# Router logits from unnormalised rows, their products moved into the memory attention, and result rows added by GpSimd

## What is computed

```python
x = layer_norm(DEEPNORM_ALPHA * x + memory_cross_attention(x, mem, w_q, w_kv, w_o), ln_g[l, 1], ln_b[l, 1])
# o = softmax(q k^T / 16) v for 4 heads of 256; returns o @ w_o
s = jax.nn.sigmoid((xf @ w_router).astype(jnp.float32))        # (512, 32)
sel = s + b_router
# best of 8 groups by its two largest sel; the two best experts in that group; gates = s normalised
x = layer_norm(DEEPNORM_ALPHA * x + y, ln_g[l, 2], ln_b[l, 2])  # y: gated sum of two SwiGLU experts
```

## Time and profile before

| | us |
|---|---|
| median of 3 runs (1113.65 to 1114.56) | 1114.0 |
| the profiled execution, whole | 1116.74 |
| its span, first to last instruction | 1115.0 |
| TensorE busy | 1041.0 (93%) |
| VectorE, ScalarE, GpSimd busy | 343.8, 251.8, 95.8 |
| mean granted clock of TensorE | 0.984 |

### The profile page before, as it was taken

One profiled execution on the slowest core, in us unless ns is written; L12 is line 12 of the kernel. 1 busy time (PEld: TensorE's weight loads), 2 busy tenths in 40 slices (PEclk: granted clock), 3 DMA queues, 4 the chain that ended last, 5 costly groups with the idle time before them and its releaser, 6 DMA issues.

```text
span 1115.0 us, 15720 instructions
## 1 busy us (share of the span) xinstructions
PE 1041.0 (93%) x6594; PEld 521.4 (47%) x6594; DVE 343.8 (31%) x730; ACT 251.8 (23%) x510; POOL 95.8 (9%) x137
## 2 busy tenths in 40 slices
PE   9999999999998999999999899999999999788896
PEld 4444455567655554566544743333333333233332
DVE  0179622334555645203216511111111111011105
ACT  2431122234445520013402111111111111011123
POOL 2000100000000000100000211111111111111111
PEclk9999999999999999999999899999999999999999
DMA  8012320221122150543833899999999999999994
GB/s 279 26 54 76 114 77 2 77 71 42 43 77 97 58 189 1 214 203 129 301 133 125 309 393 419 423 419 421 419 418 422 414 416 416 414 417 416 420 416 175
DMA packets 57462, 265.73 MB, mean 238 GB/s; under 512 B 7122, under 2 KB 8274, under 8 KB 32560
## 3 DMA queue, kind: packets, MB, share of 16 engines
q1 hardware_dynamic: 51200, 255.49, 57.8%
q0 software_dynamic: 4960, 8.15, 2.0%
q10 hardware_dynamic: 1232, 1.08, 0.3%
HBM read 256.56 MB, written 16.25 MB: 245 GB/s over the span
## 4 chain that ended last, share of the span: by engine, by line
PE 42%; DMA 9%; DVE 5%; ACT 2%; issue 1%; DVEq 0%; SPq 0%; ACTq 0%
PE cpair L2042 10%; PE bank L2052 8%; PE tpair L2042 6%; PE bank L1882 2%; PE bank L1862 2%; DMA keys<-in_w_exp_up 2%; DMA ring<-in_w_exp_down 2%; DMA ar<-in_w_exp_down 2%; DMA xT<-in_w_exp_up 2%; DMA ring<-in_w_exp_up 2%; PE bank L2024 2%; DVE hs L2471 2%; PE tpair L1882 1%; ACT hs L2268 1%; PE bank L1855 1%; PE cpair L1882 1%
## 5 line engine op out<-in xcount | busy, mean ns | idle before, releaser
L2042 PE MATMUL cpair<-ring,xgT 128*64 128x512 f32 x344 | 113.5, 593 | 5.0 <-DMA avq<-in_w_exp_up 2.6
L2471 DVE TENSOR_TENSOR hs<-cpair,hs 64x512 f32<-64x512 f32 x21 | 14.6, 693 | 247.8 <-ACT hs L2268 247.8
L2268 ACT ACTIVATE hs<-cpair 64x512 f32<-64x512 f32 x21 | 12.4, 589 | 230.9 <-PE cpair L2042 230.9
L2042 PEld LDWEIGHTS cpair<-ring,xgT 128*64 128x64 f32 x344 | 35.4, 137 | 55.8 <-issue 55.8
L922 PE MATMUL bank<-xT,ring 128*128 128x512 f32 x128 | 60.9, 606 | 0.0
L1785 POOL DMA_INDIRECT y_rows<-ye,tabs x30 | 30.6, 1018 | 349.0 <-ACT xgt L2274 329.7
L2042 PE MATMUL tpair<-ring,xgT 128*64 128x512 f32 x168 | 58.2, 614 | 2.2 <-DMA ring<-in_w_exp_up 2.2
L365 PE MATMUL bank<-xT,ring 128*128 128x512 f32 x112 | 48.5, 593 | 0.0
L2471 DVE TENSOR_TENSOR hs<-tpair,hs 64x512 f32<-64x512 f32 x11 | 7.6, 693 | 132.1 <-ACT hs L2268 132.1
L941 PE MATMUL tpair<-ring,mixT 128*128 128x512 f32 x96 | 42.0, 593 | 0.0
L1012 ACT ACTIVATE pcb<-tpair 128x512 f32<-128x512 f32 (+1 forms) x32 | 17.4, 544 | 78.9 <-DVE pcb L1180 78.9
(11 more groups left out here) (478 smaller groups left out, 1919.9 us busy)
## 6 DMA issues: line engine op xcount, KB each, us to landing
ring<-in_w_exp_up SPq DMA_DIRECT2D x32, 1024.0 KB, 10.1
ring<-in_w_exp_gate SPq DMA_DIRECT2D x32, 1024.0 KB, 10.3
ring<-in_w_exp_down SPq DMA_DIRECT2D x16, 1024.0 KB, 10.7
ring<-in_w_in SPq DMA_DIRECT2D x6, 2048.0 KB, 8.1
ring<-in_w_mem_kv SPq DMA_DIRECT2D x4, 2048.0 KB, 10.4
opening<-in_w_exp_gate SPq DMA_DIRECT2D x8, 1024.0 KB, 10.4
mixT<-in_w_exp_down SPq DMA_DIRECT2D x8, 1024.0 KB, 10.4
mixT<-in_w_exp_gate SPq DMA_DIRECT2D x8, 1024.0 KB
```

Source lines behind the costliest of these rows:

```text
L2042: last = nc.tensor.matmul(bank[b][m * CAP:(m + 1) * CAP, :], xgT[:, j, h, :], w(m, h)[:, j * DE:(j + 1) * DE], start=(k == 0), stop=(k == ...
L2268: nc.scalar.activation(sil, bank[1 + e % 3][0:CAP, :], ACT.Silu).then_inc(sil_done, 1)
L2471: V.tensor_tensor(hb, bank[1 + e % 3][CAP:P, :], sil, ALU.mult).then_inc(h_done, 1)
```

## The change

- Router: x2 W = rstd (v W' - mean * sum(W')) + b W, with v the row before the norm and W' = g W. v is alpha x1 + o Wo, so v W' = alpha (x1 W') + o (Wo W'). `x1 W'` and `Wo W'` are computed in the memory attention, after units 3, 4, 6 and 7 (`router_at`), from a transposed copy of Wo that is a new input; `o (Wo W')` stands between the result products; mean and deviation are applied to 32 logits a row on VectorE. GpSimd makes W' and its sums.
- The rows are no longer turned, copied and multiplied after the norm. Their last scaling is on VectorE for row tiles 0 to 2, on ScalarE and GpSimd for tile 3.
- Router weights and the transposed Wo are loaded earlier on SyncE's queue, pieces 1 to 4 and 6 later.
- The unread matmuls ahead of the rank product are 38 instead of 26.
- In the last stage GpSimd sums the rows of all four tiles, TensorE adds one term instead of two for tiles 2 and 3, tile by tile, and ScalarE's and VectorE's order is changed.

The core of the diff:

```diff
@@ SyncE, memory()
                     load_group(sp, GMO)
-                    for n in range(7):
-                        load_piece(sp, n)
+                    sp.dma_start(wr[:, :, :], w_router.rearrange("(p k) n -> p k n", k=KT)).then_inc(router_here, 16)
+                    sp.dma_start(brb[:, :], b_router.rearrange("(a n) -> a n", a=1).to_broadcast([P, NE]))\
+                        .then_inc(router_here, 16)
+                    for k in range(0, KT, 2):
+                        sp.dma_start(w_o_t[:, k:k + 2, :], w_mem_o_t.rearrange("(p k) i -> p k i", k=KT)[:, k:k + 2, :])\
+                            .then_inc(w_o_here, 16)
+                    load_piece(sp, 0)
+                    load_piece(sp, 5)
                     load_group(sp, GMO + 1, (qm_full, 4))
                     sp.wait_ge(qm_full, 8)
                     load_piece(sp, 7)
                     load_piece(sp, 8)
+                    sp.wait_ge(vt_full, 2)
+                    for n in range(1, 5):
+                        load_piece(sp, n)
+                    sp.wait_ge(rt_full, 2)
+                    load_piece(sp, 6)
@@ GpSimd, routing()
+                    pool.wait_ge(router_here, 32)
+                    for h, name in enumerate(("n2_g", "n2_b")):
+                        at = ROWS[name][0]
+                        link(pool, pool.tensor_tensor(gb_w[:, h, :, :], wr[:, :, :],
+                                                      cols[:, at:at + KT].unsqueeze(2).to_broadcast([P, KT, NE]), ALU.mult))
...
-                    pool.wait_ge(lg_full, 2)
-                    link(pool, pool.memset(xgt[:, 0, :], 0.0))
+                    pool.wait_ge(scaled3, 1)
+                    pool.tensor_tensor(x1[:, NT - 1, :], x1[:, NT - 1, :], ln_gb[:, 1, :], ALU.add).then_inc(n2.shifted, 1)
                     pool.wait_ge(oh_both, 2)
@@ GpSimd, experts()
-                    for t in range(2):
+                    for t in range(NT):
                         pool.wait_ge(y_read[t], 16)
                         pool.tensor_tensor(x3[t], yb[t][:, 0, :], yb[t][:, 1, :], ALU.add).then_inc(rows_sum, 1)
@@ TensorE
+                def router_products(to, weights, moving):
+
+                    for i in range(2):
+                        for g in range(4):
+                            k = 4 * i + g
+                            last = nc.tensor.matmul(to[g * NE:(g + 1) * NE, :], weights[:, k, :], moving(k),
+                                                    start=(i == 0), stop=(i == 1))
+                    return last
...
+                    def router_step(n):
+                        if n == 0:
+                            pe.wait_ge(gw_done, 1)
+                            pe.wait_ge(route_consts, 1)
+                            pe.wait_ge(qm_read, 5)
+                            router_products(bank[6], g_w, lambda k: x1T[:, k, :]).then_inc(rt_full, 1)
+                        elif n < 3:
+                            i = n - 1
+                            pe.wait_ge(w_o_here, 64)
+                            pe.wait_ge(rt_read, n)
+                            router_products(bank[6], g_w, lambda k: w_o_t[:, k, i * 512:(i + 1) * 512]).then_inc(vt_full, 1)
+                        else:
+                            pe.wait_ge(rt_read, 3)
+                            for c in range(KT):
+                                last = nc.tensor.matmul(bank[6][:, c * NE:(c + 1) * NE], vt[:, c * P:(c + 1) * P], ident4[:, :],
+                                                        start=True, stop=True)
+                            last.then_inc(rt_full, 1)
...
                     for hf, t in [(0, 2), (0, 3), (1, 0), (1, 1), (1, 2), (1, 3)]:
-                        if hf and t == NT - 1:
-                            tokens(0)
                         out_part(hf, t, range(KT)).then_inc(mo2_full, 1)
-                    tokens(1)
-                    tokens(2)
...
+                        if (hf, t) == (0, 2):
+                            pe.wait_ge(mpt_read, 2 * MH)
+                            router_products(bank[7], v_w, lambda k: omT[:, k, :]).then_inc(lg_full, 1)
+                        if (hf, t) == (0, 3):
+                            pe.wait_ge(lg_read, 1)
+                            parts_summed(6).then_inc(lt_full, 1)
+                        if (hf, t) == (1, 1):
+                            pe.wait_ge(raw_here, 1)
+                    pe.wait_ge(n2.added, 3)
                     unread(UNREAD[0])
@@ TensorE, rows(t)
-                        pe.wait_ge(y_read[t], 16)
+                        pe.wait_ge(rows_sum, t + 1)
                         for hf in range(2):
-                            for k in range(TOP_K):
-                                last = nc.tensor.matmul(bank[acc[t][hf]][:, :], ident[:, :],
-                                                        yb[t][:, k, hf * 512:(hf + 1) * 512],
-                                                        start=False, stop=(k == TOP_K - 1))
-                            last.then_inc(acc_full, 1)
+                            nc.tensor.matmul(bank[acc[t][hf]][:, :], ident[:, :], x3[t][:, hf * 512:(hf + 1) * 512],
+                                             start=False, stop=True).then_inc(acc_full, 1)
@@ ScalarE, routing()
+                    for t in range(NT):
                         n2.root(act, t)
                     act.wait_ge(router_here, 32)
                     nc.scalar.activation(t1c[:, 3, 0:1], brb[:, 0:1], ACT.Sigmoid)
+                    act.wait_ge(logit_done, NT)
+                    nc.scalar.activation(sa[:, 1, :, :].rearrange("p t e -> p (t e)"), sa[:, 0, :, :].rearrange("p t e -> p (t e)"),
+                                         ACT.Sigmoid, scale=-1.0).then_inc(aff_done, 1)
+                    act.wait_ge(n2.centred, NT)
+                    nc.scalar.activation(x1[:, NT - 1, :], x1[:, NT - 1, :], ACT.Copy, scale=rstd[:, NT - 1:NT])\
+                        .then_inc(scaled3, 1)
@@ VectorE, routing()
+                        link(dve, nc.vector.scalar_tensor_tensor(sa[:, 0, t, :], g_sum, mv[:, t, 0:1], raw[:, t, :],
+                                                                 ALU.mult, ALU.subtract))
+                        dve.wait_ge(n2.rooted, t + 1)
+                        link(dve, nc.vector.reciprocal(rstd[:, t:t + 1], rstd[:, t:t + 1]))
+                        nc.vector.scalar_tensor_tensor(sa[:, 0, t, :], sa[:, 0, t, :], rstd[:, t:t + 1], b_sum,
+                                                       ALU.mult, ALU.subtract).then_inc(logit_done, 1)
```

More of the change, by code:

```diff
@@ L1938, in memory @@
                         if n % NT == 0:
+                            pe.wait_ge(rt_read, 4)
                             product(n // NT - 2)
                 def routing():
-                    def tokens(t):
-                        pe.wait_ge(n2.shifted, t + 1)
-                        for hf in range(2):
-                            for k in range(4):
-                                c = 4 * hf + k
-                                last = nc.tensor.transpose(bank[2 * t + hf][:, k * P:(k + 1) * P],
-                                                           x1[:, t, c:D:KT], ident[:, :])
-                            last.then_inc(t2_full, 1)
-                    def logits(b, cs):
-                        for i in range(2):
-                            for g in range(4):
-                                k = 4 * i + g
-                                last = nc.tensor.matmul(bank[b][g * NE:(g + 1) * NE, cs], wr[:, k, :], x2T[k // 4][:, k % 4, cs],
-                                                        start=(i == 0), stop=(i == 1))
-                        last.then_inc(lg_full, 1)
                     def unread(count):
@@ L1964, in unread, with parts_summed @@
                             nc.tensor.matmul(bank[2][:, 0:P], ident[:, :], ident[:, :], start=True, stop=True)
-                    def parts_summed(b, t):
-                        return nc.tensor.matmul(bank[b][:, t * NE:(t + 1) * NE], lg[:, t * P:(t + 1) * P],
-                                                ident4[:, :], start=True, stop=True)
+                    def parts_summed(b):
+                        for t in range(NT):
+                            for n, part in enumerate((lg, lgx)):
+                                nc.tensor.matmul(bank[b][:, t * NE:(t + 1) * NE], part[:, t * P:(t + 1) * P],
+                                                 ident4[:, :], start=(n == 0), stop=(n == 1))
+                        return nc.tensor.matmul(bank[b][:, NT * NE:(NT + 2) * NE], ones[:, :],
+                                                gb_sum[:, :, :].rearrange("p h e -> p (h e)"), start=True, stop=True)
                     pe.wait_ge(mp_done, len(mu_))
@@ L2170, in experts @@
                         combined(t, 1, False)
-                    for t in (2, 3):
                         rows(t)
@@ L2240, in routing @@
-                    for t in range(NT - 1):
-                        n2.root(act, t)
```

(17 more changed lines are left out.)

124 lines of the change are left out of this document (67 added, 57 removed).

## The result

In runs taken in turn on the same chip the changed kernel took a median of 1121.9 us (1118.3 to 1125.0) and the kernel before 1114.8 (1113.7 to 1117.6). The ratio is 1.0053, interval 1.0036 to 1.0069: slower by 0.53%. A second session gave 1.0045, interval 1.0031 to 1.0060 (1119.8 against 1114.7 us). The forecast of 1120.3 us is a ratio of 1.0057. The total came out nearly right, but in part by luck: two errors of opposite sign stand in it, as will be seen.

A forecast was written before the change was run, and what follows sets the result against it. TensorE was taken to bound the kernel up to T0, then a chain of waits up to E0, then a fixed-length expert stage. Terms +9.3 - 1.3 - 1.7 = +6.3 on 1114.0 gave 1120.3 us, range 1115.0 to 1123.6.

The forecast's parts named there:

- Part 1: Memory attention and result stage, until the last result product ends (T0): router products on TensorE add 9.3 us, bounds 8.9, 10.4.
- Part 2: From the last result product's end to the router's affinities: affinities ready 4.2 us earlier.
- Part 3: After the affinities: GpSimd's shift of row tile 3 holds a VectorE step with two SBUF inputs, +2.0 us, bounds 0, 2.35.
- Part 4: Before the rank product: TensorE idles 3.6 us, its clock falls and slows that product, +0.9 us, bounds 0 and 2.6.
- rival (b): Clock falls so that rank product and token table are both slow: 1.7 us more, 1122.0 us; chance 0.14 with Rival (d).
- From T0 to E0: From the last result product's end (T0) to the turning of expert 0's rows (E0): 1.3 us gained, bounds 4.2 gained, 0.6 lost.
- Part 5: Last stage: GpSimd sums all four row tiles, TensorE adds less; end 1.7 us earlier, bounds 0.8 and 2.8.
- Rival (d): Last stage: GpSimd's last sum comes too late and TensorE waits; gain 0, 1122.0 us; chance 0.14 with rival (b).
- What was to cost nothing: Early loads of transposed Wo and router weights, later pieces, GpSimd's products with W', 16 more parameter columns: no added time.

The follow-up runs named there:

- shift_on_dve: The changed kernel with row tile 3's scale and shift on VectorE during its wait for the rank product, without ScalarE's scaling and GpSimd's sum; ratio 1.0016 to the kernel before.

## Why the prediction was right, and where not

**Part 1, TensorE before T0 (+9.3; measured +10.5).** The mechanism held: TensorE is the bound, shown by the doubled products. The size was off by 1.2, a little above the upper bound of 10.4 (and the bounds are loose: 5.9 and 7.2 with 2.9 make 8.8 and 10.1, not 8.9 and 10.4). What I left out is the price of standing between products of another shape. I priced a product as twice the distance between its halves, 1.71, which is right for a product that follows its like. The three in the attention took 0.14 more each until the next start, 0.4 in all, and the old products beside the new ones lost 0.44. The 0.5 that I took off for TensorE's waits for pm, as the earlier trace rows shows one, was right in kind: two long waits and a short one went, as forecast, and gave 0.40 back. The turning of vt took 1.71 in place of 1.8. The result stage was forecast at 2.9 and took 3.18: its product of 512 columns cost 1.85 in place of 1.7, the nine small ones 1.96 in place of 2.1, and the rest lies in what stands around them.

**Part 2, affinities (-4.2; measured -4.41).** Right. ScalarE's root and table load come as forecast, and the Sigmoid begins 1.41 us after the load's start, where I had 1.60; that is the difference. VectorE's pass over tile 3 just fits in front: it ends at 618.67, when the affinities' add begins, and the Sigmoid ends within 0.03 of it.

**Part 3, the exclusion (+2.0; measured +2.03).** Right, with its mechanism: one step with two SBUF inputs took 2.23 in place of 0.19, and it is gone when GpSimd's pass is gone. The inference from the earlier trace rows, where GpSimd had waited for VectorE, to the other direction was the riskiest of the prediction. By the Trainium skill (SBUF — State Buffer, Who interferes with whom) it needed none, since it says that either engine blocks the other; the rows agree, with that number in the changed kernel and, in `shift_on_dve`, with GpSimd's sum of 1.60 that takes 0.61 alone.

**Part 4, the clock (+0.9; measured +1.87).** The idle time (3.6, found 3.74) and the fall were right, and keeping TensorE busy takes the whole cost back. The size was too low by 1.0 in this execution. In the forecast I let the slow clock meet the rank product only. It also met the twelve unread products between rank product and token table, and a part of the token table. Behind the row table showed such a run of unread products at the slow clock, 3.35 us for 16 records, so the trace had the hint. A single number is also the wrong form for this term, since the same pause cost 0.96, 1.74, 1.87 and 3.01 us in four executions. The last is the case of rival (b), with rank product and token table slow, and lies above my upper bound of 2.6; the first is my 0.9. Which of them comes, the pause doesn't say.

**From T0 to E0 (-1.3; measured -0.7)** follows from these.

**Part 5, the tail (-1.7; measured -2.0).** Tail of the changed kernel, GpSimd's last sum and VectorE's passes:

```profile
1100.64 1.28 DVE L2591 SCALAR_TENSOR_TENSOR ring<-opening,blkones,xT 128x1024 f32<-128x1024 f32 x1
1100.89 3.25 POOL L1868 TENSOR_TENSOR ring<-ring 128x1024 f32<-128x1024 f32 x1 [0.16 <-DMA ring<-y_rows]
...
1103.42 1.80 DVE L2591 SCALAR_TENSOR_TENSOR ring<-ring,blkones,xT 128x1024 f32<-128x1024 f32 x1
```

The last sum of GpSimd waits for the first centring pass (3.25 in place of 2.35) and holds the second (1.80 in place of 1.28). I had 1.0 for that hold, and it was 0.5. From VectorE's last addition of expert rows (at 1093.07 before, 1096.99 after) the end comes 2.3 us earlier, and 0.3 is lost again between the last refill and that addition. Rival (d) falls: the tail gains 2.0 here, and 2.5 without the router.

**What was to cost nothing** did so: with all early loads and the later pieces, and no new arithmetic, the stretch up to the first product with the values is the 27.36 of before. The loads themselves go out before that stretch, and there TensorE takes 29.73 us from its second to its sixth group of query products (467.02 to 496.75), and 29.74 in the kernel before.

**What wasn't in the sum:** the 3.0 us of the expert stream. The parts that I did name come to +7.8 in the trace, 1.5 more than forecast; the stream gave 3.0 back. So the time of 1120.3 was hit with two errors of opposite sign, part 1 and the clock on one side and the stream on the other. That they nearly cancel is luck: nothing in the prediction ties them together. The sum up to E0 was +8.0 by forecast and +9.8 by the trace.

## What to carry to other kernels

Arithmetic that is moved off a latency chain onto an engine that is the bound costs its full time there: 10.5 us of TensorE paid for 4.4 us of earlier affinities. The waits that it could fill gave back 0.4, and the change between kinds of products took as much. Look for the two things that a shortened chain lays bare: an engine that now idles long enough for its clock to fall, and a helper engine's long pass beside another's short steps with two SBUF inputs. And a change in two parts is to be timed in two parts: the tail alone is 0.16% faster than the kernel before (interval 0.05% to 0.27%), four kernels with the same tail and an idle addition or another order of loads are 0.27% to 0.33% faster, and that gain was buried under the router. Last, a pass that is put into an engine's wait can look free at the slow clock: VectorE's shift of tile 3 cost 0.9 us when the clock stayed up.

## What the runs showed of the hardware

- VectorE and GpSimd exclude each other in both directions, for whole instructions: VectorE's step of 32 elements took 2.23 in place of 0.19 us beside GpSimd's pass, and GpSimd's of 256 elements 1.60 in place of 0.61 beside VectorE's. A step of VectorE with one input that began inside GpSimd's pass took its usual 0.19 (at 622.47, with GpSimd's pass from 622.24 to 624.64).
- Ahead of the rank product TensorE's granted clock fell to 0.50 (1.2 GHz) behind pauses of 1.72, 3.74, 3.75 and 5.11 us, in all six executions that have them, and stayed at 1.00 over the pauses of 0.37 to 0.72 us in the other eight. The same pause of 3.74 or 3.75 us cost 0.96 to 3.01 us up to the token table in four executions.
- At the start of the memory attention, behind the same pauses of 1.82 and 0.73 us, the clock fell in six of 14 executions and stayed in eight. The fall cost 1.4 to 3.1 us (43.64 to 45.31 against 42.26 from the request for w_mem_q to that for w_mem_o).
- A product of eight matmuls in four column groups over 512 columns costs 1.71 us behind its like and 1.85 between products of another shape, whose neighbours lose 0.06 to 0.11 in each place besides.
- An unread product ahead of a dependent step is no longer free once the clock has fallen: twelve records took 2.91 us in place of 1.58.
- The same stream of 168 pieces took 433 us in one family of kernels and 436 in another, at steps of 2.43 or 2.48 us a piece, and none of loads, order, a further input or tile places brought the difference by itself.
